# One transformer layer in float32: a written drain of the first stage, a moved maximum product and wider diagonal maxima

## The reference, cut to what matters

```python
def reference(x, mem, ...):                      # x (1, 2048, 1024), everything float32
    h = rms_norm(x, g_attn);  proj = h @ w_in    # cut into q, k, v of three head groups
    # A: 8 query / 2 key heads, window of own chunk and the one before (64 frames each), sinks
    # B: 4 heads over low-rank latents, mask: key_chunk <= query_chunk
    # M: 4 heads over 256 memory tokens
    s = where(key_chunk <= query_chunk, q @ k.T * scale, -1e30);  p = softmax(s);  o = p @ v
    x = x + concat(A, B, M) @ w_o
    return x + square(relu(rms_norm(x) @ w_ff1)) @ w_ff2
```

## Time and profile before

| | busy us | share of the span | instructions |
|---|---|---|---|
| TensorE | 2132.9 | 97% | 10024 |
| VectorE | 1434.9 | 65% | 2095 |
| ScalarE | 1035.1 | 47% | 1863 |
| GpSimd | 1094.0 | 50% | 898 |

### The profile page before, as it was taken

The page is one execution under the profiler, slowest core; times in us unless marked ns, Lnnn a source line. Parts: engine busy times, 40 slices in busy tenths (PEclk is TensorE's granted clock), DMA queues, the critical chain, the costliest instruction groups (busy, mean ns, idle before and its releaser), DMA issues. The chain is left out here.

```text
span 2200.0 us, 31733 instructions
## 1 busy us (share of the span) xinstructions
PE 2132.9 (97%) x10024; PEld 1756.6 (80%) x10024; DVE 1434.9 (65%) x2095; ACT 1035.1 (47%) x1863; POOL 1094.0 (50%) x898
## 2 busy tenths in 40 slices
PE   8999999879999999989999989999999999999999
PEld 6899999667777777767888878888888888888887
DVE  5788888868765656477777787677644564354463
ACT  6566666547666666654333443333423232222221
POOL 2665665734456666657656666666445720020220
PEclk9999999989999999999999999999999999999999
DMA  6142242678557655575444564444577752233363
GB/s 241 38 120 81 81 120 63 196 221 245 181 179 212 196 184 171 195 237 187 157 156 144 169 243 158 157 147 149 187 253 273 243 206 106 96 134 135 136 225 117
DMA packets 291403, 370.64 MB, mean 168 GB/s; under 512 B 27280, under 2 KB 186192, under 8 KB 289488
## 3 DMA queue, kind: packets, MB, share of 16 engines
q1 hardware_dynamic: 291280, 369.08, 51.8%
HBM read 244.07 MB, written 124.93 MB: 168 GB/s over the span
## 5 line engine op out<-in xcount | busy, mean ns | idle before, releaser
L128 PE MATMUL bank<-f_t_hi,f_w_hi 128*128 128x512 f32 x896 | 350.4, 391 | 9.4 <-issue 5.9
L128 PE MATMUL bank<-f_t_lo,f_w_hi 128*128 128x512 f32 x896 | 349.3, 390 | 0.0
L128 PE MATMUL bank<-f_t_hi,f_w_lo 128*128 128x512 f32 x896 | 349.1, 390 | 0.0
L128 PE MATMUL bank<-f_w_lo,f_a_hi 128*128 128x512 f32 x896 | 348.6, 389 | 0.0
L128 PE MATMUL bank<-f_w_hi,f_a_hi 128*128 128x512 f32 x896 | 348.6, 389 | 0.0
L128 PE MATMUL bank<-f_w_hi,f_a_lo 128*128 128x512 f32 x896 | 348.5, 389 | 0.0
L2337 POOL TENSOR_TENSOR a_p_lo<-a_prob,a_p_hi 128x512 fp32r<-128x512 f32 (+1 forms) x192 | 233.6, 1226 | 189.4 <-DVE a_p_hi L2478 92.1
L128 PEld LDWEIGHTS bank<-f_t_hi,f_w_hi 128*128 128x128 f32 x896 | 168.5, 188 | 48.1 <-issue 10.7
L1680 POOL TENSOR_TENSOR f_r<-f_r,f_y 128x512 f32<-128x512 f32 x24 | 42.0, 1789 | 324.5 <-DMA f_r<-s_x 324.5
L1778 DVE TENSOR_TENSOR f_a_lo<-f_a_raw,f_a_hi 128x1024 fp32r<-128x1024 f32 x112 | 155.8, 1391 | 72.1 <-ACT f_a_hi L1705 71.6
L128 PEld LDWEIGHTS bank<-f_t_hi,f_w_lo 128*128 128x128 f32 x896 | 168.6, 188 | 35.2
(11 more groups left out here) (323 smaller groups left out, 4861.4 us busy)
## 6 DMA issues: line engine op xcount, KB each, us to landing
f_a_raw<-s_aop SPq DMA_DIRECT2D x112, 512.0 KB, 4.3
w_raw<-in_w_ff SPq DMA_DIRECT2D x64, 512.0 KB, 5.2
s_aop<-f_a SPq DMA_DIRECT2D x128, 256.0 KB, 4.4
s_aop<-f_s SPq DMA_DIRECT2D x96, 256.0 KB, 2.4
f_w_raw<-in_w_ff SPq DMA_DIRECT2D x64, 256.0 KB, 5.4
f_t_raw<-s_hop SPq DMA_DIRECT2D x14, 1024.0 KB, 9.0
f_r<-in_w_ff SPq DMA_DIRECT2D x48, 256.0 KB, 6.1
a_vals<-s_v SPq DMA_DIRECT2D x40, 264.0 KB, 4.6
```

The source lines that it names most:

```text
L128: ins = pe.matmul(out, a, b, start=(first and j == 0), stop=(last and j == n - 1))
```

## The change

It has three parts.

**A drain of its own.** `steps` now runs bodies up to NT - 1 and then one `drain(ta, tb, tc)` for the last three tiles (13, 14, 15), in which each engine's order is written out. The repeated pieces of the bodies become functions. In step NT - 1 TensorE turns the queries of tile 14 before the last cut and its latents inside that cut; SP fetches `w_o` and the first mixed tiles at the head of the step. VectorE takes three of four weight remainders and mixed tiles 0 and 2, GpSimd one and tiles 1 and 3 (before: two and one, two and three). The first early visit is split into its eight pairs of `hi` products for both halves (`first_highs`) and its eight `lo` products (`first_lows`). The last tile's latents go to buffers of their own (`last_hi`, `last_lo`). The core of the diff, with TensorE's drain and its changed last step:

```diff
-            for s in range(NT - 4, NT + 3):
+            for s in range(NT - 4, NT):
                 body(0, s)
+            drain(*(tile_at(0, n) for n in range(NT - 3, NT)))
...
+                def drain(ta, tb, tc):
+                    score(tb)
+                    weigh(ta)
+                    turn_mem(tc, pB[:, 256:512])
+                    pe.wait_ge(n_act, NT * N_ACT)
+                    E["first_highs"](pe, y_bank)
+                    wait(pe, w_dve, tb.n * W_DVE + 4)
+                    turn_lat(tc, pG[:, 512:])
+                    wait(pe, l_dve, (ta.n + 1) * L_DVE)
+                    wait(pe, l_act, (tb.n + 1) * L_ACT)
+                    turn_latents(ta, 0, pC)
+                    E["first_lows"](pe, y_bank)
+                    wait(pe, out_made, (ta.n + 1) * 2)
+                    turn_latents(ta, 1, pD)
+                    turn_heads(tc)
+                    turn_keys(tc)
+                    for a in range(2):
+                        E["half"](pe, y_bank[a], 1, a)
...
+                    turn_probs(tb)
...
+                    score(tc)
+                    weigh(tb)
+                    E["half"](pe, y_bank[0], 2, 0)
...
+                    turn_latents(tb, 0, pC)
...
+                    turn_latents(tb, 1, pD)
+                    E["half"](pe, y_bank[1], 2, 1)
+                    E["half"](pe, y_bank[0], 3, 0)
...
+                    turn_probs(tc)
+                    E["half"](pe, y_bank[1], 3, 1)
...
+                    turn_latents(tc, 0, pC)
+                    turn_latents(tc, 1, pG)
+                    weigh(tc)
...
                     if s == NT - 1:
+                        turn_heads(t)
+                        def inside():
...
+                            turn_lat(t, pC)
+                        cut(t0, 2, inside)
...
+                        turn_keys(t)
```

```diff
-                dve.tensor_reduce(part_max[0:CHUNK, q, ch:ch + 1], src[0:CHUNK, 0:w - CHUNK], AX.X, ALU.max)
-                dve.tensor_reduce(part_max[CHUNK:, q, ch:ch + 1], src[CHUNK:, 0:w], AX.X, ALU.max).then_inc(max_done, 1)
+                dve.tensor_reduce(part_max[:, q, ch + 1:ch + 2], src[:, 0:w - CHUNK], AX.X, ALU.max)
+                dve.tensor_reduce(part_max[CHUNK:, q, 0:1], src[CHUNK:, w - CHUNK:w], AX.X, ALU.max).then_inc(max_done, 1)
...
+            if U == 0:
+                dve.wait_ge(const_made, 2)
...
-        dve.wait_ge(const_made, 10)
...
+        pool.memset(neg_max[:, :, :], 0.0).then_inc(const_made, 1)
+        pool.wait_ge(const_made, 1)
+        pool.memset(part_max[0:CHUNK, :, 0:1], LOWEST).then_inc(const_made, 1)
+        pool.wait_ge(const_made, 2)
         pool.memset(zeros[:, :], 0.0).then_inc(const_made, 1)
```

More of the change, by code:

```diff
@@ L698, in prepare, with store_v @@
                     O["sync_stores"](sp)
-                def body(i, s):
[L701 to L704, removed]
-                            E["load_swa"](sp, v)
[L706 to L718, removed]
+                def store_v(t):
+                    wait(sp, lv_lo_done, t.n + 1)
+                    sp.dma_start(S["v"][:, :, bass.ds(t.n, 1), :, :].rearrange("p h a e d -> p h (a e d)"), lv[:, :, :, :].bitcast(F32).rearrange("p h e d -> p h (e d)")).then_inc(lv_stored, 16)
@@ L736, in body @@
                     t = tile_at(i, s - 1)
                     if live(t, NT):
[L738 to L741, removed]
+                        store_m(t)
@@ L802, in body @@
                         st = Chain(pool, n_pool, t.n, N_POOL)
[L803 to L827, removed]
+                        head_roots(t, st)
+                        head_gains(t, st)
+                        split_values(t)
                     t = tile_at(i, s + 1)
@@ new lines, in prob_sums @@
+                def prob_sums(t, w):
+                    wait(dve, exp_done, t.n + 1)
+                    if first(t):
+                        dve.memset(prob[:, 0:HP, CHUNK:KEYS], 0.0).then_inc(const_made, 1)
+                        wait(dve, const_made, FILLS + 1)
+                    wait(dve, scaled, t.n)
+                    w.link(dve.tensor_reduce(sums[:, :], prob[:, :, 0:KEYS + 1], AX.X, ALU.add))
+                    w.link(dve.reciprocal(sums[:, :], sums[:, :]))
+                    w.end()
@@ L1214, in up, with score @@
                         ins.then_inc(up_made, 1)
+                def score(t):
+                    wait(pe, h_dve, (t.n + 1) * H_DVE)
+                    wait(pe, h_act, (t.n + 1) * H_ACT)
+                    for b in range(NB8):
+                        n, hp = b // HP, b % HP
+                        g = hp * 2 // SG
+                        pick = slice(0, 3, 2) if n == 0 else slice(0, 2)
+                        out = pG[:, b * KEYS:(b + 1) * KEYS].rearrange("p (a k) -> p a k", a=2)
+                        q = q_st[:, n, 2 * hp:2 * hp + 2, :].rearrange("d h q -> d (h q)")
+                        pe.matmul(out, q, k_hi[t.b][:, g, pick, :], start=True, stop=False)
+                        ins = pe.matmul(out, q, k_lo[t.b][:, g, pick, :], start=False, stop=True)
+                        if b == NB8 - 1:
+                            ins.then_inc(scored, 1)
+                        up(t, b)
+                    up(t, 8)
```

914 lines of the change are left out of this document (573 added, 341 removed).

## The result

The changed kernel takes 2187.89 us (median of 4 runs, 2187.09 to 2188.25), the kernel before in the same session 2200.65 (4 runs, 2199.94 to 2202.42): a ratio of 0.9939, with a 95% interval of 0.9926 to 0.9953. The forecast was 2185.5 in 2177 to 2193.5. The profiled span fell from 2200.0 to 2185.3 us.

A forecast was written before the change was run, and what follows sets the result against it. TensorE, busy 97% of the span, was taken as the bound, with VectorE the drain's floor once reordered. Savings of 6.9 (drain), 4.0 (attention's start) and 4.0 (rest), 14.9 us, gave 2185.5 us from the 2200.38 median; range 2177 to 2193.5.

The forecast's parts named there:

- the wait for tile 14's key remainders: TensorE in the drain: this wait, 4.95 us before, was to fall under 2 us.
- the start of attention: First memset to first score product: earlier memset, shorter diagonal maxima and a moved product save 4.0 us, bounds 2.1 and 5.
- the waits for maxima: TensorE behind the first score product: its waits for VectorE's maxima were to total below 1.5 us.
- The floor of the drain: End of the first stage: with TensorE's order repaired, VectorE's work sets the length; 6.9 us saved to the barrier.
- It removes no product: New drain: same products, only reordered and shared out anew; costs counted from 392.24 us, 6.9 us saved.
- A clock drop there costs nothing while VectorE sets the pace: Drain, TensorE's 3.4 us stand for tile 13's probability remainders: half clock there was to cost no time.
- The rest of attention: Behind the first score product: fewer waits for maxima and a kept clock save 4.0 us, bounds -1 and 7.
- hidden under TensorE: Other 15 causal units: VectorE loses 1.2 us each, 18 us, taken as already covered by TensorE's work.
- The port pair (2): Drain: VectorE and GpSimd locking SBUF ports, or tight hand-overs, keep 6.6 us idle; 8.6 saved in all, 2192; chance 0.24.
- SP's queue (3): Drain: 21 first loads ahead of tile 13's latent stores delay ScalarE; 12 us slower, 2212; chance 0.05.
- More (1): Drain and attention: VectorE meets GpSimd less and the clock holds; 22 us saved, 2178; chance 0.17.
- no change (4): Whole kernel: longer tail and the walk's errors eat the gain, little of the start counts; about 2200; chance 0.04.

The follow-up runs named there:

- both sides: Changed kernel with TensorE's waits before transposes in their former order: 2185.61 us; kernel before with only the new order of waits: 2201.24 us.
- the drain alone: Kernel before with only the new drain, attention as before: 2199.09 us, ratio 0.9995.
- the gains ahead: Changed kernel, but GpSimd multiplies tile 15's heads by their gains before taking the fourth weight remainder: 2184.26 us.
- the constants' order: Kernel before, with only the attention constant VectorE needs set first and VectorE's wait moved to the first negation: 2198.09 us, ratio 0.9986.
- the old maxima: Changed kernel, but the two reductions of a diagonal tile are split by rows as before: 2193.27 us.
- the product unmoved: Changed kernel, but the second maximum product of a slot stands before the score product again: 2191.68 us.
- the first mix remainder earlier: Changed kernel with old loop waits and GpSimd's gains first, plus VectorE's first mix remainder before tile 15's head norms: 2183.65 us, against 2182.70 without it.

## Why the prediction was right, and where not

The time was right by luck in part, since errors of opposite sign cancel: drain and loop gave 3.6 us less than forecast, the rest of attention 4.4 us more. Of the signs named in the prediction, the wait for tile 14's key remainders (0.49 us), VectorE's idle time (3.4) and the start of attention (5.77) came as said; the first memset came at 452.93 instead of 448 to 449, and the waits for maxima were 1.7 us, not below 1.5.

- **The floor of the drain** held: VectorE ends it. Its busy time is 50.1 us (forecast 49.3) and its idle time 3.4 (2.3); the tail 4.8 (4.7). From the begin of the drain to the release that is 58.4 us instead of 63.3: 4.9 saved, not 6.9. The terms that were mis-sized are VectorE's busy time (0.8 us) and its idle time (1.1 us). The first is about what its meetings with GpSimd grew by: an estimate from the rows, each long instruction against the same one at its shortest, gives 5.9 us of excess here (memory query 2.2, first mix remainder 1.3, `p_lturn` at 431.47 1.1, third weight remainder 0.8) and 4.8 before (`p_stat_l` 2.0 and 1.0, mix remainder 1.5).
- **The step "It removes no product", with the costs counted from 392 us on,** failed: I looked for the price of the new drain in the drain. The rewritten bodies changed the order of TensorE's waits in the counted loop, 1.6 us ahead of it, shown from both sides. Of 6.9 us 3.3 are left; by its median the drain alone gives 1.6, by its pieces in the profile 3.2 (4.8 - 1.6), at the edge of its interval (3.1 faster to 1.1 slower). What takes the difference is not settled; A scatters by as much.
- **"A clock drop there costs nothing while VectorE sets the pace"** was wrong. It costs nothing while the early products are early enough: with a long half clock VectorE waited 1.4 and 0.8 us for them, 0.3 and 0.5 in the two profiles of the changed kernel, none with the gains ahead.
- **The start of attention** was right: E fell by 3.85 us (4.0), 2.11 of it by the constants' order (2.1); with the old maxima 0.4 us come back (0.7), with the product unmoved 0.9.
- **The rest of attention** is the term that was too small: 4.0 forecast, 8.4 measured, outside its bounds of -1 to 7. The waits for maxima fell from 3.8 to 1.7 us, 2.1 of the 3.8 I had. The nine products behind the longest wait (from 603.73 to 607.20 before, from 594.37 to 596.45 now) take 1.4 us less, for they keep the full clock, as hoped (1.7). What the forecast had at nothing is the wait for ScalarE's copy of the maxima, 1.5 us; it comes back with the old maxima, and not with the product unmoved. The other 3.4 us are in neither of these: shifts of 0.3 to 1.1 us, most of them at a score product behind maxima. I had called 18 us of VectorE "hidden under TensorE"; with the old maxima 4.2 us come back, with the product unmoved 1.9.
- **The rivals.** The port pair (2) is real; one order of GpSimd gives back 1.4 us, 0.6 of it busy time of VectorE. It did not decide. SP's queue (3) acted as described, but small: the loads ran to 429.5 us, ScalarE waited 2.85 us and VectorE 0.5 of them. More (1) and no change (4) did not come.

## What to carry to other kernels

When code is rewritten into functions, compare the order of waits in every loop it touches, not only where the work moves: a quarter of a microsecond a step is invisible in a list of waits, and visible as a step length. Cut both spans at common marks before explaining a median, since errors can add up to a right forecast; and compare a stretch with the same work in the other kernel, not with the same microseconds. Work of another engine counts as hidden only if it is hidden at each hand-over, not on the average, and the hand-over can lie one engine further on, as ScalarE's copy did here.

## What was not expected of the hardware

- With another order of waits in TensorE's queue, and a register instruction behind one of them, the gap ahead of a transpose was 0.38 us instead of 0.20, and the profile names nothing that was waited for.
- A VectorE operation on 8 columns took 1.21 us instead of 0.16 beside a GpSimd subtraction, while the 1024-column subtraction from PSUM just ahead of it took its usual 1.21 us.
- GpSimd's power of 16 columns (3.02 us, from 401.58 in the changed kernel; spans on GpSimd are rough) excluded nobody: three short VectorE operations with both inputs in SBUF, from 401.56 to 402.75, took their usual 0.28 to 0.42 us each. The profiles with the gains ahead and with the first mix remainder earlier show the same.
